# Output gates of an mLSTM mixer: their projection moved from the projections' program into the recurrence's program

## The reference

```python
h  = modulate(rmsnorm(x))                       # 512 latent tokens (and 256 of context) x 1024
qk, v, o, gates = h @ w_in                      # query and key, value, output gate, input/forget gates of 2 directions
q, k = silu(conv3(qk))                          # depthwise convolution over 3 tokens
# 8 heads, forward and backward: exponentially weighted sums of v over the tokens, with
# running maxima for stability, taken in blocks of 128 tokens:
y = (masked decay * scores) @ v + (weighted q) @ state;  y = y / max(|norm|, exp(-max))
y = rmsnorm_per_head(y) * out_g * sigmoid(o)    # the output gate is needed only here
x = x + cgt * (y @ w_out)
```

## Time and profile before

| | us |
|---|---|
| median of 3 runs (lowest, highest) | 4022.14 (4019.82, 4028.83) |
| the profiled execution, its own time | 4022.15 |
| its span, first to last instruction | 4020.7 |
| PE busy | 3890.9 (97%) |
| DVE busy | 1985.0 (49%) |
| ACT busy | 1399.3 (35%) |
| mean granted TensorE clock, of 2.4 GHz | 0.96 |

### The profile page before, as it was taken

One profiled execution on the slowest core, in us unless ns is written; L12 is line 12 of the kernel. 1 busy time (PEld: TensorE's weight loads), 2 busy tenths in 40 slices (PEclk: granted clock), 3 DMA queues, 4 the chain that ended last, 5 costly groups with the idle time before them and its releaser, 6 DMA issues.

```text
span 4020.7 us, 46292 instructions
## 1 busy us (share of the span) xinstructions
PE 3890.9 (97%) x18628; PEld 3142.8 (78%) x18628; DVE 1985.0 (49%) x3158; ACT 1399.3 (35%) x2336; POOL 478.4 (12%) x411
## 2 busy tenths in 40 slices
PE   7999999999999999999999989999999999989999
PEld 4867777888887866788888866888768887658888
DVE  2345556645456245544443358434444445574343
ACT  2235443313125223323332247322332223593222
POOL 0510024740000010000010000200011000101000
PEclk8999999999999976999999999999999999899999
DMA  4310012333332110233333322333322332103332
GB/s 182 103 35 1 1 39 88 126 100 128 100 121 75 63 33 11 84 99 97 98 95 97 98 84 79 94 99 95 95 74 90 99 95 89 32 1 98 96 100 89
DMA packets 105829, 330.08 MB, mean 82 GB/s; under 512 B 11537, under 2 KB 13201, under 8 KB 105617
## 3 DMA queue, kind: packets, MB, share of 16 engines
q1 hardware_dynamic: 100944, 317.24, 25.1%
q10 hardware_dynamic: 4672, 9.89, 0.7%
HBM read 324.99 MB, written 2.10 MB: 81 GB/s over the span
## 4 chain that ended last, share of the span: by engine, by line
PE 84%; DVE 5%; ACT 2%; issue 1%; POOL 0%; DMA 0%; ACTq 0%; DVEq 0%; POOLq 0%
PE ps L540 23%; PE ps L541 23%; PE ps L542 23%; PE ps L1366 3%; PE ps L1351 2%; PE ps L1339 1%; PE ps L1336 1%; PE ps L1340 1%; PE ps L2437 1%; PE ps L2435 1%; PE ps L1243 1%; PE ps L1244 1%; PE ps L1245 1%; DVE t L707 1%; DVE t L723 1%
## 5 line engine op out<-in xcount | busy, mean ns | idle before, releaser
L540 PE MATMUL ps<-t 128*128 128x512 f32 (+1 forms) x4640 | 1762.4, 380 | 31.5 <-DVE t L723 14.2
L541 PE MATMUL ps<-t 128*128 128x512 f32 (+1 forms) x4640 | 1739.3, 375 | 0.0
L542 PE MATMUL ps<-t 128*128 128x512 f32 (+1 forms) x4640 | 1738.0, 375 | 0.0
L540 PEld LDWEIGHTS ps<-t 128*128 128x128 f32 x4640 | 881.4, 190 | 224.1 <-issue 37.6
L541 PEld LDWEIGHTS ps<-t 128*128 128x128 f32 x4640 | 882.4, 190 | 156.9 <-issue 7.0
L542 PEld LDWEIGHTS ps<-t 128*128 128x128 f32 x4640 | 880.8, 190 | 155.6
L297 DVE TENSOR_TENSOR t<-t 128x1024 fp32r<-128x1024 f32 (+1 forms) x517 | 647.9, 1254 | 479.6 <-ACT t L288 478.3
L288 ACT ACTIVATE t<-t 128x1024 fp32r<-128x1024 f32 (+1 forms) x517 | 533.2, 1031 | 776.3 <-PE ps L542 691.2
L1107 POOL TENSOR_TENSOR t<-t 128x512 f32<-128x512 f32 x88 | 113.9, 1294 | 1219.7 <-ACT t L1094 1219.7
L481 POOL TENSOR_SCALAR t<-t 128x512 f32<-128x512 f32 x77 | 145.7, 1892 | 488.2 <-DVE t L462 488.2
L1137 DVE SCALAR_TENSOR_TENSOR t<-ps,t 128x512 f32<-128x512 f32 x96 | 66.4, 692 | 239.4 <-PE ps L542 239.4
(11 more groups left out here) (340 smaller groups left out, 3433.3 us busy)
## 6 DMA issues: line engine op xcount, KB each, us to landing
t<-w_s_up SPq DMA_DIRECT2D x176, 512.0 KB, 3.6
t<-w_up SPq DMA_DIRECT2D x88, 512.0 KB, 3.7
t<-w_ada SPq DMA_DIRECT2D x160, 256.0 KB, 2.9
t<-w_s_down SPq DMA_DIRECT2D x64, 512.0 KB, 3.6
t<-w_down SPq DMA_DIRECT2D x32, 512.0 KB, 3.7
t<-w_s_down SPq DMA_DIRECT2D x32, 384.0 KB, 3.0
t<-w_ada SPq DMA_DIRECT2D x16, 512.0 KB, 16.3
t<-w_rec_in SPq DMA_DIRECT2D x16, 512.0 KB, 3.5
```

Of the source, the lines that this page charges most:

```text
L540: k.T.matmul(out, wh, hh, start=(i == 0), stop=False)
L541: k.T.matmul(out, wh, hl, start=False, stop=False)
L542: ins = k.T.matmul(out, wl, hh, start=False, stop=(i == len(kts) - 1))
```

## The change

The output gates' projection leaves the projections' program. In the recurrence's program a new `pe_gate(step)` stands at the end of each of the 40 steps: five steps take one chunk of `ml_o`, with 2, 2, 1, 2 and 1 k tiles, which is 6, 6, 3, 6 and 3 matmuls. All accumulate in bank 5. `act_gate(step)` stands at the head of each step; at every fifth it splits the chunk two ahead, waits for the 8 k tiles before it and evicts bank 5. Up to step 25 the eviction is a Copy, and the Sigmoid of these five results is taken later in place, at steps 31 to 35; from step 30 on it is a Sigmoid. The low split of DVE stands at the head of the same steps. The gates now lie in the slots of keys and queries that are no longer needed, in place of `O`, so `H`, the normed input, lives on through the recurrence, and its tile is used again for `MX`. The state updates get one bank in place of two, so they go in three parts (x = 5, 6, 7, of 3, 3 and 2 blocks) in place of two (of 4 and 4). The tiny matmuls and their copies follow the values' projection directly. `KB`, `KW`, `SQ` and one of the states move to tiles that are free by then.

```diff
@@ projections, PE
-                for m in range(8):
-                    w = st.operand(c0 + 17 + m, "ml_o", m)
-                    b, before = k.banks.take(ok.at(m + 1))
-                    bank[("o", m)] = b
                     k.pe.wait_ge(before)
-                    dense(k, b, w, H.k, range(KT)).then_inc(od.sem, 1)
-                    st.used[c0 + 17 + m] = od.at(m + 1)
-                    if m == 0:
-                        for d in range(2):
...
@@ projections, ACT
-                for m in range(8):
-                    st.split_hi(c0 + 19 + m)
-                    k.act.wait_ge(od.at(m + 1))
-                    k.A.activation(O[:, m, :], bank[("o", m)], ACT.Sigmoid).then_inc(ok.sem, 1)
@@ recurrence, PE
-                    if x in (5, 6):
-                        d = x - 5
+                    if x > 4:
                         k.pe.wait_ge(kw.at(p + 1))
-                        k.pe.wait_ge(cs.at(8 * p + 4 * d))
-                        for j in range(4):
+                        k.pe.wait_ge(cs.at(8 * p + 3 * (x - 5)))
+                        for n, (d, j) in enumerate(updates[x - 5]):
...
+                def pe_gate(step):
+
+                    m, at = divmod(step, 5)
+                    k0, k1 = (0, 2, 4, 5, 7, 8)[at:at + 2]
+                    w = o_weights[m] if at else o_weights.setdefault(m, st.operand(c0 + 17 + m, "ml_o", m))
+                    if at == 0:
+                        k.pe.wait_ge(ok.at(m))
+                    for kt in range(k0, k1):
+                        (wh, wl), (hh, hl) = w.k(kt), H.k(kt)
+                        k.T.matmul(k.ps[:, 5, :], wh, hh, start=(kt == 0), stop=False)
+                        k.T.matmul(k.ps[:, 5, :], wh, hl, start=False, stop=False)
+                        ins = k.T.matmul(k.ps[:, 5, :], wl, hh, start=False, stop=(kt == 7))
+                    if at == 4:
+                        ins.then_inc(od.sem, 1)
+                        st.used[c0 + 17 + m] = od.at(m + 1)
...
+                def act_gate(step):
+
+                    m, at = divmod(step, 5)
+                    if at == 0:
+                        if m < 8:
+                            st.split_hi(c0 + 19 + m)
+                        if m:
+                            k.act.wait_ge(od.at(m))
+                            k.act.wait_ge(sd.at((m + 1) // 2))
+                            k.A.activation(gate(m - 1), k.ps[:, 5, :], ACT.Copy if step < 29 else ACT.Sigmoid).then_inc(ok.sem, 1)
+                    if 31 <= step < 36:
+                        v = gate(step - 31)
+                        k.act.wait_ge(ok.at(step - 30))
+                        k.A.activation(v, v, ACT.Sigmoid).then_inc(og.sem, 1)
...
@@ the loop over the steps, PE
                             if p >= 0:
                                 pe_unit(p, x)
+                            pe_gate(8 * (p + 1) + x)
@@ the loop over the steps, ACT
                         for x in range(8):
+                            act_gate(8 * (p + 1) + x)
                             if p < 3:
                                 act_prepare(p + 1, x)
...
                     act_square(31)
+                    act_gate(40)
@@ the loop over the steps, DVE
                         for x in range(8):
+                            if (8 * (p + 1) + x) % 5 == 0:
+                                st.split_lo(c0 + 19 + (8 * (p + 1) + x) // 5)
                             if p < 3:
                                 dve_prepare(p + 1, x)
@@ behind the recurrence
-            MX = k.alloc_pair(scope, KT, NL)
+            MX = H
...
-                                                 in1=O[:, kt, :], op0=ALU.mult, op1=ALU.mult).then_inc(md.sem, 1)
+                                                 in1=gate(kt), op0=ALU.mult, op1=ALU.mult).then_inc(md.sem, 1)
```

More of the change, by code:

```diff
@@ L2119, in odd_mixer @@
         V = k.alloc(base, 6, 8 * 129)
-        O = k.alloc(base, 8, NL)
-        G = k.alloc(base, NT)
-        F = k.alloc(base, NT)
+        GF = k.alloc(base, 2 * NT)
+        G, F = GF[:, 0:NT], GF[:, NT:2 * NT]
         M = k.alloc(base, NL)
@@ L2131, in odd_mixer, with gate @@
         masks = [CM[:, 128:256], CM[:, 0:128]]
+        def gate(m):
+            return KK[:, m // 2, 0:NL] if m % 2 else QQ[:, m // 2, :]
         selm = CM[:, 256:1280].rearrange("p (h n) -> p h n", h=8)
@@ L2179, in pe_program @@
                 rows.pe()
-                for m in range(8):
-                    w = st.operand(c0 + 17 + m, "ml_o", m)
-                    b, before = k.banks.take(ok.at(m + 1))
-                    bank[("o", m)] = b
+                for d in range(2):
+                    pr = slice(32 * d, 32 * d + 8)
+                    b, before = k.banks.take(ck.at(2 * d + 2))
+                    bank[("col", d)] = b
                     k.pe.wait_ge(before)
-                    dense(k, b, w, H.k, range(KT)).then_inc(od.sem, 1)
-                    st.used[c0 + 17 + m] = od.at(m + 1)
-                    if m == 0:
-                        for d in range(2):
[L2189 to L2204, removed]
@@ new lines, in pe_program @@
+                    k.pe.wait_ge(da.at(4 * d + 10))
+                    k.pe.wait_ge(t_cm)
+                    cols = [G[pr, NC + 128 * q:NC + 128 * q + 128] for q in range(4)]
+                    cols += [F[pr, NC + 128 * q:NC + 128 * q + 128] for q in range(4)]
+                    cols += [GATE[pr, 128 * q:128 * q + 128] for q in range(6)]
+                    for c, src in enumerate(cols):
+                        k.T.matmul(b[:, 8 * c:8 * c + 8], src, k.ident[pr, 32 * d:32 * d + 8], start=True, stop=True)
@@ L2206, in act_program @@
+                    for p in range(4):
+                        ins = k.T.matmul(b[:, 112 + 4 * p:116 + 4 * p], pairs(p)[pr, :], EDGE[pr, 8:12], start=True, stop=True)
+                    ins.then_inc(cd.sem, 1)
             def act_program():
@@ L2336, in dve_program @@
                 rows.dve(lambda x: edges(x) if x < 2 else None)
[L2337 to L2345, removed]
+                for d in range(2):
+                    k.dve.wait_ge(cd.at(d + 1))
+                    k.V.tensor_copy(COL[:, d, :, :].rearrange("p b c -> p (b c)"), bank[("col", d)][:, 0:112])\
+                        .then_inc(ck.sem, 1)
+                    k.V.tensor_copy(DL[:, :, d, :], bank[("col", d)][:, 112:128].rearrange("p (a b) -> p a b", a=4))\
+                        .then_inc(ck.sem, 1)
             def pool_program():
@@ L2437, in pe_unit @@
                         ins = k.T.matmul(b[:, 129 * d:129 * d + 129], QW[r, p % 2, d, 128 * q:128 * q + 128],
-                                         ST[r, p % 2, d, q if d == 0 else 3 - q, :], start=False, stop=True)
+                                         ST[p % 2][r, d, q if d == 0 else 3 - q, :], start=False, stop=True)
                     ins.then_inc(un.sem, 1)
@@ L2522, in dve_prepare @@
                                                      op1=ALU.mult).then_inc(pr.sem, 1)
[L2523 to L2527, removed]
+                    if x > 4:
+                        k.dve.wait_ge(ud.at(3 * p + x - 4))
+                        for n, (d, j) in enumerate(updates[x - 5]):
+                            u = k.ps[:, 4, 129 * n:129 * n + 129]
                             if j == 0:
-                                k.V.tensor_copy(ST[:, p % 2, d, 0, :], u).then_inc(cs.sem, 1)
+                                k.V.tensor_copy(ST[p % 2][:, d, 0, :], u).then_inc(cs.sem, 1)
                                 continue
@@ L2556, in dve_program @@
                 def dve_program():
-                    for t in [t_o, h_free, t_cm]:
+                    for t in [t_col, h_free, t_cm]:
                         k.dve.wait_ge(t)
@@ L2605, in dve_program @@
                 scaled.dve()
-                for t in inner_free:
+                for t in inner_free + t_o:
                     k.dve.wait_ge(t)
```

38 lines of the change are left out of this document (22 added, 16 removed).

## The result

The changed kernel takes 3996.99 us (median of five, 3981.57 to 3998.88) against 4021.46 us (4017.25 to 4028.83) before: a ratio of 0.9932 with a 95% interval of 0.991 to 0.9954. Predicted were 3995 us, in 3974 to 4018.

A forecast was written before the change was run, and what follows sets the result against it. The prediction took PE's own program and its clock to bound the recurrence. Its terms, -45.7 - 0.3 + 18.2 + 0.6 = -27.2 us, took 4022.15 us to 3995 us, range 3974 to 4018.

The forecast's parts named there:

- Step 1: Before the recurrence: the dense chunks of the output gates' projection go, -45.7 us.
- Step 2: Tiny matmuls before the recurrence: they stay, with the clock falling at another point, -0.3 us, bounds -2.8 to +3.5.
- Step 3: Recurrence's PE work if the clock is always high: 86.4 as before, 44.0 gate matmuls, 6 boundaries, 136.4 us.
- Step 4: Recurrence's clock: low for 37 us, 16.4 us more; stage 152.8 against 134.6, +18.2 us, bounds +1.8 to +73.4.
- Step 5: Other engines' work in the recurrence: hidden, cost about 0, 13 us without cover; last eviction at the tail, +0.6 us.
- A: Recurrence: the gates do not raise the clock, low in 78% of the stage as before; 4050 us, chance 0.13.
- B: Recurrence: the clock is high nearly throughout; 3979 us, chance 0.17.
- C: Recurrence: the clock falls once in each of three rounds with preparation, low for 20 us; 4012 us, chance 0.17.
- D: Recurrence: ACT evicts the one bank late, PE stands 1.85 us at each of seven chunks; 4008 us, chance 0.08.

The follow-up runs named there:

- e12: The changed kernel with k tiles reordered (first chunk in four steps), ACT's eviction before its split, and DVE's low split behind its unit: 3983.2 us.
- e1: The changed kernel run again with nothing edited, to profile a second execution (the second profile): 3996.54 us.
- e3: The changed kernel with each chunk's 24 gate matmuls all in the last of its five steps: 4037.31 us.
- e2: The changed kernel with 184 of the 192 gate matmuls left out: 4005.11 us.
- e5: The kernel before with its state updates in three parts on one bank and nothing else changed: 4035.99 us.
- e7: The changed kernel with ACT evicting bank 5 before it splits the next chunk: 3991.32 us.
- e8: The changed kernel with the edits of e6 and e7 together: 4010.76 us.
- e4: The changed kernel with every gate matmul issued twice, 192 more: 4026.78 us.
- e6: The changed kernel with 2 or 3 k tiles at steps with 8-row matmuls in the middle rounds, mostly one at update steps: 3985.03 us.
- e9: The changed kernel with 1 or 2 k tiles in every step, reordered so middle-round steps with 8-row matmuls have two: 3988.9 us.

## Why the prediction was right, point by point

- **What bounds the stage** (PE's program times the clock): right. The stages of three kernels with the same 744 matmuls took 138.5, 154.8 and 196.8 us at 0.97, 0.88 and 0.65 (e12, e1, e3); less their low time x 0.444 they come to 135.3, 138.1 and 136.4.
- **Step 1**, -45.7: exact, since nothing of it comes back as idle time elsewhere.
- **Step 2**, -0.3 for the tiny matmuls: -0.9 and -1.1, within the bounds.
- **Step 3**, 136.4 us if always high: the second profile holds 154.8 - 37.7 x 0.444 = 138.1, the first 140.9 - 6.7 x 0.444 = 137.9. Two terms were low: boundaries 8 us and not 6 (the upper bound held), and 3.7 us of waits for the one bank where it had none. The other terms were a little high. The three us of waits in the first round are gone, as the gates fill them. And the recurrence's own work was taken at 86.4 - 3 = 83.4, where the stage before gives 134.6 - 105.8 x 0.444 - 5.1 of idle time = 82.5. An estimate from these, 82.5 + 44.0 + 8 + 3.7 = 138.2, closes.
- **Step 4**, 37 us low at a mean of 0.88: 37.7 at 0.88 in the usual execution, but made up otherwise. Forecast were 15 us until the first rise and two falls of 11; found were 3.7 until the first rise, and six falls, two of 10.2 us and four of 3.4, 34 us in all. The start was too dear and the falls too few. That the sum agreed is luck: the errors went against each other. "Three were seen in the recurrence" is a misreading of the trace: the clock fell there four times, at 1448.2, 1465.2, 1496.0 and 1530.1, the first of them in the round that only prepares. The rate "3 rises in 7 runs", read from the kernel before, was a weak guide: e2 has the updates and no rise at all, e3 has denser bursts and is at 0.65. That six matmuls in most steps work and 24 in one step don't was not forecast.
- **Step 5**: the three-part updates were priced at nothing and cost the old recurrence 14 us (e5), which this kernel doesn't pay only because its clock is held otherwise. The wait for the bank was priced at 0, with 13 us as the other end: 3.7 us in the trace, most of it at step 5, where ACT still has the first round's exponentials in its list, a step that no row of the kernel before shows. 0.5 us of it stand at step 30, where ACT loads a function table (1.28 us at 1507.0) ahead of the first eviction with Sigmoid, which the forecast did not have. e7 removed half of it and put as long a wait elsewhere; its 5 us came with fewer low microseconds.
- **The rivals.** A (low as before) is wrong for this kernel, but e3 shows that it is near: it keeps all the matmuls and loses the clock. B came true in one execution in five, and again in one of the four of e1_again. C named three steps that did fall (9, 12 and 17), and gave each 20 us where 10.2, 3.4 and 10.2 passed; it missed steps 25 and 26. D is real and small.

Left open: why one execution in four or five escapes the falls, and what exactly in the work raises the clock. The runs show that spread gates hold it up, and that updates, 8-row matmuls and single bursts of 24 don't. Whether PE's waits of one to three us set off some of the falls is open as well: in most kernels a fall stands at such a wait (e8, e12), but not in e4, and others stand where PE has no gap (e1).

## What to carry to other kernels

Read the granted clock of each stage beside PE's busy share: a stage can be 96% busy and run at half rate (e2), and dense matmuls that must be done anyway are then worth moving into it, since they cost their high-clock time and speed up all that stands beside them. Spread them over all steps, not in bursts (e3); an order with more of them beside the smallest matmuls (e6, e12) gave the lowest medians, but an even one (e9) can't be told from it. When an edit moves one engine's list (eviction before split), follow the two engines behind it: alone it gained a little, and with another order of k tiles it cost 26 us, 21 of them through the clock (e8).

## What was not expected of the hardware

- Less work was slower: 184 dense matmuls taken out cost 8.6 us (4005.11 against 3996.54 us), at 0.50 through 161.4 us with PE busy in 154.75.
- The same matmuls in bursts of 24 instead of 3 or 6 cost 41 us (4037.31 against 3996.54 us). In both kernels the stage less 0.444 of its low time comes to 136 to 138 us.
- The clock depends on what went before: the last round's work, with three gate matmuls in most steps, ran at 1.00 in 18.9 us in e6, and at 0.50 in 33.5 us in e8, where the clock fell 1.8 us behind a wait of 1.34 us, just before that round.
- A change between float32 and split matmuls costs some 0.1 us each way at the high clock (0.34 and 0.32 us against a pitch of 0.23).
